# A streaming encoder layer: the sample's queries, keys and values of all head pairs multiplied ahead of attention

## The reference

```python
z = rms_norm(x, g) @ w_in          # q latent 256 | kv latent 128 | rotary key 32 | u 1024 | gate_a | gate_b
q = (rms_norm(c_q) @ w_q_b).reshape(b, t, 16, 96)            # 64 plain + 32 rotary per head
lat_all = concatenate([past_lat, rms_norm(c_kv)])
kv = (lat_all @ w_kv_b).reshape(b, n_k, 16, 128)             # 64 key + 64 value per head
k_nope, v = rms_norm(kv[..., :64]), kv[..., 64:]
attn = chunk_causal_mla(q_nope, q_rope, k_nope, kr_all, v)   # block-causal softmax attention
mixed = sigmoid(gate_a) * attn + sigmoid(gate_b) * rg_lru(conv(u))
x = x + mixed @ w_out
x = x + (silu(conv(gate)) * conv(val)) @ w_down              # gate, val = rms_norm(x) @ w_up
```

## Time and profile before

| | |
|---|---|
| median of 3 runs | 874.24 us (871.04 to 875.2) |
| profiled execution, span from first to last instruction | 872.8 us; the profile gives no other time of its own |
| busy: TensorE, VectorE, ScalarE, GpSimd | 852.5, 568.6, 365.7, 192.9 us |
| moved by DMA | 63.73 MB, 73 GB/s on average |

### The profile page before, as it was taken

One profiled execution on the slowest core, in us unless ns is written; L12 is line 12 of the kernel. 1 busy time (PEld: TensorE's weight loads), 2 busy tenths in 40 slices (PEclk: granted clock), 3 DMA queues, 4 the chain that ended last, 5 costly groups with the idle time before them and its releaser, 6 DMA issues.

```text
span 872.8 us, 16689 instructions
## 1 busy us (share of the span) xinstructions
PE 852.5 (98%) x6522; PEld 817.2 (94%) x6522; DVE 568.6 (65%) x998; ACT 365.7 (42%) x608; POOL 192.9 (22%) x206
## 2 busy tenths in 40 slices
PE   5999999899999999999999999999999999999998
PEld 5999898789999899877999999999999999999998
DVE  5586678867675676887656888778777876222121
ACT  5534959655655466556245221222212221122121
POOL 4021123202021121121140333323333234010000
PEclk8999999899999999999999999999999999999999
DMA  8433311131120101100223233232322323233321
GB/s 245 116 90 95 89 49 38 40 80 38 28 54 24 53 25 29 50 1 26 73 75 95 75 94 96 72 96 74 94 81 87 94 68 93 82 105 99 104 56 39
DMA packets 114466, 63.73 MB, mean 73 GB/s; under 512 B 7660, under 2 KB 112878, under 8 KB 114412
## 3 DMA queue, kind: packets, MB, share of 16 engines
q1 hardware_dynamic: 112428, 59.25, 24.0%
q0 software_dynamic: 1936, 3.70, 1.7%
q10 hardware_dynamic: 48, 0.02, 0.0%
HBM read 59.85 MB, written 2.70 MB: 72 GB/s over the span
## 4 chain that ended last, share of the span: by engine, by line
PE 88%; ACT 6%; DVE 3%; issue 2%; DMA 0%; POOL 0%; SPq 0%; ACTq 0%; DVEq 0%; POOLq 0%
PE PS L1612 49%; PE PS L1758 9%; PE PS L1841 6%; PE PS L1775 4%; PE PS L1813 4%; PE PS L1651 3%; PE PS L1717 2%; PE PS L1795 2%; PE PS L2045 2%; PE PS L1713 2%; PE PS L1749 2%; PE PS L1739 1%; PE PS L1680 1%; PE PS L1624 1%; PE PS L1820 1%
## 5 line engine op out<-in xcount | busy, mean ns | idle before, releaser
L668 ACT ACTIVATE w_hi<-w_raw 128x1024 fp32r<-128x1024 f32 (+2 forms) x102 | 105.5, 1035 | 316.5 <-PE PS L1612 301.4
L1101 DVE TENSOR_TENSOR w_lo<-w_raw,w_hi 128x1024 fp32r<-128x1024 f32 (+2 forms) x102 | 124.8, 1224 | 114.5 <-ACT w_hi L668 114.3
L1612 PE MATMUL PS<-x2h,w_hi 128*128 128x274 f32 x704 | 147.6, 291 | 0.0
L1612 PE MATMUL PS<-x2h,w_lo 128*128 128x274 f32 x704 | 147.0, 290 | 0.0
L1612 PE MATMUL PS<-x2l,w_hi 128*128 128x274 f32 x704 | 146.9, 290 | 0.0
L1612 PEld LDWEIGHTS PS<-x2l,w_hi 128*128 128x128 f32 x704 | 112.0, 189 | 0.0
L1612 PEld LDWEIGHTS PS<-x2h,w_hi 128*128 128x128 f32 x704 | 111.9, 189 | 0.1
L1612 PEld LDWEIGHTS PS<-x2h,w_lo 128*128 128x128 f32 x704 | 111.4, 189 | 0.0
L630 POOL TENSOR_TENSOR uct<-uct 128x548 f32<-128x548 f32 x22 | 30.2, 1373 | 176.4 <-DVE uct L1565 176.4
L1612 PE MATMUL PS<-hh,w_hi 128*128 128x274 f32 x308 | 64.7, 291 | 0.0
L1612 PE MATMUL PS<-hh,w_lo 128*128 128x274 f32 x308 | 64.6, 291 | 0.0
(11 more groups left out here) (291 smaller groups left out, 1851.2 us busy)
## 6 DMA issues: line engine op xcount, KB each, us to landing
w_raw<-in_w_up_dram SPq DMA_DIRECT2D x44, 512.0 KB, 3.9
w_raw<-in_w_in_dram SPq DMA_DIRECT2D x24, 512.0 KB, 3.9
w_raw<-in_w_down_dram SPq DMA_DIRECT2D x16, 512.0 KB, 4.3
w_raw<-in_w_out_dram SPq DMA_DIRECT2D x8, 512.0 KB, 4.3
w_raw<-in_w_down_dram SPq DMA_DIRECT2D x8, 384.0 KB, 4.0
xnat<-in_x_prompt_dram SPq DMA_DIRECT2D x4, 512.0 KB, 5.4
w_raw<-in_w_in_dram SPq DMA_DIRECT2D x4, 416.0 KB, 7.4
wq<-in_w_q_b_dram SPq DMA_DIRECT2D x8, 192.0 KB, 2.5
```

Source lines behind the costliest of these rows:

```text
L668: nc.scalar.activation(hi[:, slot % 2, 0:n], raw[:, slot % 4, 0:n], ACT.Copy).then_inc(s_hi, 1)
L1101: tt(lo[:, slot % 2, 0:n], raw[:, slot % 4, 0:n], hi[:, slot % 2, 0:n].bitcast(F32), ALU.subtract).then_inc(s_lo, 1)
L1612: last = mm(PS[:, 2 * rank + j, 0:HT], w[:, slot % 2, cols], x[:, k0 + k, j * HT:(j + 1) * HT], start=(k0 + k == 0 and first), stop=(k0 + ...
```

## The change

The sample's rows leave the tiles. TILES becomes (4, 4, 2, 2): two key units of four tiles, two query units of two, and two value units. In their place two calls of sample_qkv multiply the 32 sample rows by the weights of all pairs, the first call (r = 0) for pairs 0, 2, 4, 6, the second for the odd ones, four pairs at a time in column groups of 32. They stand in products g = 5 and g = 6; the keys and queries of pair 0 stay in g = 7 and 8. ScalarE evacuates each result and stores it to a new HBM tensor; before each pair it issues three DMAs that fetch the 32 rows into Kn, Qn and V. GpSimd clears the 96 other rows of the last tiles once.

```diff
-        TILES = (4, 4, 1, 2, 2, 1)
+        TILES = (4, 4, 2, 2)
+        NUNIT, NVU = 4, 2
 # SP
+            def sample_weights(r):
+                if r:
+                    sp.wait_ge(s_smul, r)
+                for k in range(NQ):
+                    sp.dma_start(swq[:, k, :, :], w_q_s[:, k, r]).then_inc(s_swin, 16)
+                sp.dma_start(swkv[:, :, :], w_kv_s[:, r]).then_inc(s_swin, 16)
             for t in range(I_IN, I_IN + 11):
                 w_in_item(t)
+                if t == I_IN + 5:
+                    sp.wait_ge(s_ss, NTT)
+                    sample_weights(0)
+            sample_weights(1)
 # GpSimd, after conv_tail(5)
+            pool.wait_ge(s_sst, 32)
+            for s in range(2):
+                nc.gpsimd.memset(Kn[s][0:LASTP, NKT - 1, :, :], 0.0)
+                nc.gpsimd.memset(Qn[s][0:LASTP, NT, :, :], 0.0).then_inc(s_sz, 1)
 # ScalarE
             def evacuate_kq(q, u, bank):
+                if u == 0:
+                    if q >= 2:
+                        act.wait_ge(s_tr, q * 5 - 5)
+                    else:
+                        act.wait_ge(s_sst, 32)
...
+                    act.dma_start(Kn[q % 2][LASTP:, NKT - 1, :, :], heads[:, 0]).then_inc(s_skq[q % 2], 16)
+                    act.dma_start(Qn[q % 2][LASTP:, NT, :, :].rearrange("p h n -> p (h n)"), rows_q[:, 0:2 * QK]).then_inc(s_skq[q % 2], 16)
+            def evacuate_sample(r):
+                act.wait_ge(s_smul, r + 1)
+                nc.scalar.activation(sqkv[:, r, 0:2 * QK], PS[:, 4, 0:2 * QK], ACT.Copy)
+                nc.scalar.activation(sqkv[:, r, 2 * QK:], PS[:, 5, 0:4 * NOPE], ACT.Copy).then_inc(s_sev, 1)
+                act.wait_ge(s_sev, r + 1)
+                act.dma_start(store[r], sqkv[:, r, :]).then_inc(s_sst, 16)
             def evacuate_v(q, u, bank):
+                if u == 0:
...
+                    act.dma_start(V[LASTP:, q % 2, NKT - 1, 0:3:2, :], heads[:, 1]).then_inc(s_svin[q % 2], 16)
 # ScalarE, squares_keys
+                act.wait_ge(s_skq[q % 2], 32 * (q // 2) + 32)
 # ScalarE, attend
-                    if kq and n < 3:
+                    if kq and n < 2:
                         evacuate_kq(p + 2, 2 * n, 0)
                         evacuate_kq(p + 2, 2 * n + 1, 1)
 # ScalarE, early stretch, after lru_exps (g == 5) and lru_mults (g == 6)
-                if 6 <= g < 9:
+                if 4 <= g < 6:
+                    evacuate_sample(g - 4)
+                if 6 <= g < 8:
                     for u in range(2):
                         evacuate_kq(0, 2 * (g - 6) + u, 4 + u)
...
-            for u in range(4, 6):
-                evacuate_kq(1, u, u - 4)
 # TensorE
+            def sample_qkv(r):
+                pe.wait_ge(s_swin, 48 * (r + 1))
+                for k in range(NQ):
+                    for g in range(4):
+                        mm(PS[g * DEC:(g + 1) * DEC, 4, 0:2 * QK], cqT[:, k, S0:S0 + DEC], swq[:, k, g, :],
+                           start=(k == 0), stop=(k == NQ - 1))
+                for g in range(4):
+                    last = mm(PS[g * DEC:(g + 1) * DEC, 5, 0:4 * NOPE], latT[:, SEQ + PAST:], swkv[:, g, :], start=True, stop=True)
+                last.then_inc(s_smul, 1)
 # TensorE, values
+                if n == 8:
+                    pe.wait_ge(s_svin[p % 2], 16 * (p // 2) + 16)
 # TensorE, attend
-                    if kq and n in (1, 2):
-                        for u in (2 * n, 2 * n + 1):
+                    if kq and n == 1:
+                        for u in (2, 3):
...
-                    for u in (1, 2):
...
-                        values_in(p + 1, u, (u + 1) % 2)
+                    values_in(p + 1, 1, 0)
 # TensorE, early stretch, before lru(g - 3)
+                if 5 <= g < 7:
+                    pe.wait_ge(s_sev, g - 4)
-                if 7 <= g < 10:
+                if 7 <= g < 9:
                     pe.wait_ge(s_kqf, 2 * (g - 6))
```

More of the change, by code:

```diff
@@ L172, in layer @@
         U = fixed("U", [P, KD, LEAD + T])
+        gates_at = place
         gates = fixed("gates", [P, 3, 2, T])
@@ L228, in layer @@
         lsq = at("lsq", [P, NTT, KVL + ROPE], zone + NTT * QL * 4)
+        NS = 2 * QK + 4 * NOPE
+        swq = at("swq", [P, NQ, 4, 2 * QK], kq_at[1])
+        swkv = at("swkv", [P, 4, 4 * NOPE], gates_at + 4 * T * 4)
+        sqkv = at("sqkv", [P, 2, NS], kq_at[0] + NKT * 2 * NOPE * 4)
+        assert kq_at[1] + NQ * 4 * 2 * QK * 4 <= wq_at and 4 * 4 * NOPE <= 2 * T and 2 * NS <= NTT * 2 * QK
+        assert kq_at[1] >= zone + NTT * (QL + KVL + ROPE) * 4
         mxh = at("mxh", [P, KD, T], xs, F32R)
@@ L331, in layer @@
         s_kq, s_kqf = sem("kq_product"), sem("kq_evacuated")
+        s_swin, s_smul, s_sev, s_sst = sem("sample_weights_in"), sem("sample_qkv_product"), sem("sample_qkv_evacuated"), sem("sample_qkv_stored")
+        s_sz = sem("sample_tiles_cleared")
+        s_skq = [sem(f"sample_kq{s}_in") for s in range(2)]
+        s_svin = [sem(f"sample_v{s}_in") for s in range(2)]
         s_v, s_vf = sem("v_product"), sem("v_evacuated")
@@ L345, in layer @@
         s_yt, s_yn, s_ysample = sem("y_transposed"), sem("y_natural"), sem("last_sample_natural")
+        store = nc.dram_tensor("sample_qkv_dram", (2, P, NS), F32, kind="Internal").ap()
         block = ctx.enter_context(nc.Block())
@@ L811, in evacuate_kq @@
             def evacuate_kq(q, u, bank):
-                act.wait_ge(s_kq, q * 6 + (u + 1))
-                if u == 0 and q >= 2:
-                    act.wait_ge(s_tr, q * 5 - 5)
+                if u == 0:
[3 more added lines that the diff above has]
+                        act.wait_ge(s_sst, 32)
+                    rows_q = store[q % 2, q // 2 * DEC:(q // 2 + 1) * DEC, :]
+                    heads = rows_q[:, 2 * QK:].rearrange("t (h c n) -> t c h n", h=2, c=2)
+                    act.dma_start(Kn[q % 2][LASTP:, NKT - 1, :, :], heads[:, 0]).then_inc(s_skq[q % 2], 16)
+                    act.dma_start(Qn[q % 2][LASTP:, NT, :, :].rearrange("p h n -> p (h n)"), rows_q[:, 0:2 * QK]).then_inc(s_skq[q % 2], 16)
+                act.wait_ge(s_kq, q * NUNIT + (u + 1))
                 tiles = TILES[u]
-                if u < 3:
+                if u < 2:
                     dst = Kn[q % 2][:, 4 * u:4 * u + tiles, :, :].rearrange("p t h n -> p (t h n)")
@@ L846, in evacuate_v @@
                     act.wait_ge(s_pv, q * 9 - 9)
[L847 to L850, removed]
+                if u == 0:
+                    heads = store[q % 2, q // 2 * DEC:(q // 2 + 1) * DEC, 2 * QK:].rearrange("t (h c n) -> t c h n", h=2, c=2)
+                    act.dma_start(V[LASTP:, q % 2, NKT - 1, 0:3:2, :], heads[:, 1]).then_inc(s_svin[q % 2], 16)
+                act.wait_ge(s_v, q * NVU + (u + 1))
+                dst = V[:, q % 2, 4 * u:4 * u + 4, 0:3:2, :]
+                nc.scalar.activation(dst, PS[:, bank, :].rearrange("p (t h n) -> p t h n", h=2, n=VD), ACT.Copy).then_inc(s_vf, 1)
             def value_ones(s):
@@ L1017, in _ @@
                 columns_left(0, v, 4 + v)
-            for u in range(3):
-                evacuate_v(0, u, (0, 1, 7)[u])
+            for u in range(NVU):
+                evacuate_v(0, u, u)
             exps(0, 0)
@@ L1745, in values_in @@
                     pe.wait_ge(s_wv[q % 2], 32 * (q // 2) + 32)
-                for a in range(TILES[u]):
-                    t = 4 * u + a
-                    k0 = t * P if t < NKT - 1 else NK - P
+                for a in range(4):
+                    k0 = (4 * u + a) * P
                     last = mm(PS[:, bank, a * P:(a + 1) * P], latT[:, k0:k0 + P], wkv[:, q % 2, 1, :], start=True, stop=True)
@@ L1909, in attend @@
                     if second and n == 8:
-                        pe.wait_ge(s_vf, 3 * (p + 1) + 1)
+                        pe.wait_ge(s_vf, NVU * (p + 1) + 1)
                         gate_half(second, 1)
                 if following:
-                    for u in (1, 2):
[L1914 to L1919, removed]
-                        values_in(p + 1, u, (u + 1) % 2)
+                    if second:
+                        pe.wait_ge(s_gf, 2 * (second - I_G) + 1)
+                    else:
+                        pe.wait_ge(s_trf, 4 * (p + 1) + 4)
+                    values_in(p + 1, 1, 0)
                 values(p, 8)
@@ L1927, in units @@
                     pe.wait_ge(s_lrui, min(g - 3, KD))
+                    if g < 7:
+                        sample_qkv(g - 5)
+                        return
                     for u in range(4) if g == NF - 1 else (2 * (g - 7), 2 * (g - 7) + 1):
                         keys_queries(int(g == NF - 1), u, 4 + u if g == NF - 1 else 4 + u % 2)
-                return units if 7 <= g < 10 or g == NF - 1 else None
+                return units if 5 <= g < 9 or g == NF - 1 else None
             pe.wait_ge(s_rs, 1)
@@ L1961, in _ @@
             pe.wait_ge(s_free, 11)
-            for u in (4, 5):
-                keys_queries(1, u, u - 4)
             for v in range(4):
```

(7 more changed lines are left out.)

37 lines of the change are left out of this document (19 added, 18 removed).

## The result

The changed kernel takes 880.88 us (median of 6 runs, 880.19 to 883.01), the kernel before beside it 874.12 (6 runs, 871.04 to 875.26): a ratio of 1.0089, 95% interval 1.0074 to 1.0105. It is slower by 6.8 us between the two medians; the interval of the ratio says 6.5 to 9.2 us. The profiled execution has a span of 878.4 us, 5.6 more than before.

What follows compares the result with a forecast made beforehand. TensorE, busy 852.5 of 872.8 us, seemed to bound the kernel, but ScalarE's work was expected to be waited for. Early stretch 5.4, pairs 1 to 5 3.5, other pairs -0.6: 8.3 us on 874.24 gives 882.5, range 871 to 888.

Steps and rivals of the forecast that it cites:

- early stretch: Everything up to attention's first exp: added products, evacuations and DMA issues cost 5.4 us, bounds 3.1 to 6.2.
- Pairs 1 to 5: Attention: TensorE stands still 1.8 us before the fifth score, awaiting ScalarE's chain; each pair 0.7 us longer, 3.5 in all.
- (1): Sixth product: the first sample_qkv call moves its end, the evacuation and ScalarE's next step by 1.1 us.
- (2): ScalarE behind lru_exps: the second sample evacuation and its DMA issue make lru(3) wait, 1.2 us in all.
- (3): evacuate_kq(0, 0) on ScalarE: two more DMA issues cost 0.9 us, making lru(4) 3.2 us late.
- (4): Ninth product: four query tiles instead of a key tile and two query tiles, 1.1 us more.
- (5): evacuate_kq(1, 0) before lru_mults: two DMA issues and four query tiles instead of two to evacuate, 0.9 + 0.2 us.
- the sign I had named: Start of attention: first exp near 160 us if the forecast holds, near 157 if it is wrong on the issues.
- TensorE's work decides: Rival, n = 1 to n = 3 of each pair: removed matmuls come through as time won, 867.6 us; chance 0.14.
- The clock: Rival: larger TensorE gaps, early and in five pairs, bring half speed; 12 us more, 894, or 885 to 888; chance 0.09.
- The groups run side by side: Denies the rival that sample_qkv's column groups run one after another, 6.6 us more in the early stretch, 889; chance 0.03.
- Half of each: Rival: early stretch at its lower bound, +3.1, pairs' gains and stalls in balance; 874.5 to 877 us, chance 0.16.

Runs made afterwards that it cites:

- e1: Changed kernel with tanh and split moved ahead of the evacuation of units 2 and 3 at n = 1, pairs 1 to 5: 872.82 us, ratio 0.9985.
- e2: Changed kernel with query unit 2 multiplied at n = 1 and unit 3 at n = 2, instead of both at n = 1: 873.7 us, ratio 1.0003.
- e3: Changed kernel without the 24 fetches of the sample's rows, which are set to zero: 881.29 us, ratio 1.0081.
- e6: Changed kernel with pair 0's units spread over three products and pair 1's unit 3 after the last product: 878.46 us, ratio 1.0045.
- e7: Changed kernel with the edits of e1, e2 and e6 together: 868.29 us, ratio 0.9936.
- e8: e7 with the first sample_qkv in the seventh product and the second in the tenth, its weights and store later: 867.51 us, ratio 0.9919.
- e5: Kernel before the change, with only tanh and split moved ahead of the evacuations at n = 1: 873.82 us, ratio 0.9996.

## Why the prediction was right

I gave 882.5 us, 871 to 888, and slower as the likeliest; it is 880.88. The kernel loses in the two places named. By places the loss is 6.6 us where I forecast 8.3, and some terms of the early stretch were priced too high. The runs as a whole (6.5 to 9.2 us) don't tell the two sums apart.

**Pairs 1 to 5: right, and shown.** Forecast: idle time of 1.8 us before the fifth score, +0.7 per pair, 3.5 in all. Found: 1.65 and 3.95 (0.74 in most pairs, 0.94 in the last). e1 and e2 show the mechanism from both sides. The margin of 0.19 us in the earlier trace rows said it: the removed work covered a chain. The fetches did fit into the gap of 0.94 us.

**Early stretch: 5.2 us forecast at the end of pair 0, 3.3 found.** (1) The first call: 1.1 forecast; from 82.56 to 83.84 it is 1.3, and lru(2) was 1.4 later. 24 instructions in 1.3 us show the column groups overlapping. On the changes of mode that the Trainium skill (TensorEngine Tiling (Array Packing), Key Properties) warns of, the trace has at most the 0.3 us by which that lies above my estimate; no run takes the changes of mode apart from the rest. (2) The second evacuation and its store behind the exps: 1.2 forecast, 1.0 found (first_tap is 2.4 us later, 95.49 against 96.92 plus the 0.98 of the starts, and the first call is 1.4 of that). lru(3) waits for the evacuation as forecast, but for 0.84 us where I had some 1.5. (3) **The step that failed**: "evacuate_kq(0, 0) issues two more, 0.9". They cost nothing (e3); lru(4) is 2.5 us late, not 3.2, and it is TensorE's own line, 3.9 late at lru(3), that sets it, not the wait for ScalarE that I had. (4) The two additional query tiles in the ninth product: 1.1 forecast, and lru(5) is another 1.1 later. e6 takes 1.3 back. (5) "0.9 + 0.2" at evacuate_kq(1, 0): the two issues at 144.49 and 144.84 lie under activations and hold ScalarE up by 0.13 us at most. In their place stood something I had not priced: ScalarE waited for pair 1's unit 3, with TensorE at its lower clock.

I had taken ScalarE's 0.46 us from the only row of that queue and let it decide five issues, 2.3 us in all. For the four of them that don't follow a wait on ScalarE's own last result the lower bound, nothing, was right or nearly so. Without those two terms of 0.9 the sum is 6.5 us, near the 6.6 found, but that agreement is luck: larger differences cancel. At the first exp 3.6 would be left and 4.35 were found, with 0.7 from the lower clock at 142 us. Pair 0 then gave 1.05 back where I had 0.2, since in the eight microseconds from the first exp on the clock stood at 0.64 and 0.94, and at 0.50 and 0.67 before. The pairs cost 0.45 more than forecast. By the sign I had named (first exp near 160, or near 157 if I am wrong on the issues) the result lies between: the first exp stands at 159.0 counted from the start before, 158.3 without the clock's 0.7.

The Trainium skill (DMA: Bandwidth & Descriptors, Issuing engines are not separate DMA queues) calls the sequencer's time for an issue usually small relative to the DMA. The trace agrees roughly: the fetches of Kn and Qn are issued in 0.31 to 0.44 us and land in 1.6 and 1.7. The size of an issue was not my mistake, then. The mistake was to add it to ScalarE's time, where it runs beside a table load or an activation.

**Rivals.** TensorE's work decides (867.6) is wrong for this kernel. Its mechanism holds in e7 and e8, where the chain is out of the way and the 1.1 us per pair come through; that their 868.29 and 867.51 lie so near its number is in part luck, since both also mend the early stretch. The clock: with idle times of 1.65 us in five pairs, the granted clock between 196 and 268 and between 300 and 336 us stays at 1.00, so that rival is refuted for pairs 1 to 5. The groups run side by side. Half of each would have needed the pairs to break even.

## What to carry to other kernels

Before taking work off a busy engine, find what that work covers: here 0.19 us of margin lay between a unit of matmuls and a chain of evacuation, tanh, split and exp on another engine, and removing 1.1 us of work cost 0.74 us per pair until the chain was reordered. A change that loses by a wait it uncovers may still beat the kernel it came from, once work that nobody waits for is moved out of the chain. Put DMA issues where an engine is still finishing earlier instructions, not behind a wait for its own last result. And compare single profiles place by place: two executions of the same work differed by 2.2 us in one stretch.

## What the hardware showed that I had not expected

**The cost of an issue depends on what stands ahead.** Under a table load or activations, two issues of 0.34 and 0.44 us cost ScalarE nothing (102.43 and 102.80; 0.13 us at most at 144.49 and 144.84). Behind a wait for the engine's own evacuation one leaves 0.40 us of idle time (at 96.92). The first is shown by e3; the second is read from the trace, and no run varied that wait alone.

**TensorE's clock differs between executions of nearly the same program.** In these windows the number after POOL's is the granted clock. From 142 to 144 us, first the changed kernel, then e3:

```profile
142.00:144.00 2.00, 2.00 (x12) 2.00 (x12) 2.00 (x4) 1.99 (x3) 1.40 (x2) 0.50 0.00 0
```

```profile
142.00:144.00 2.00, 1.90 (x17) 1.90 (x18) 2.00 (x5) 1.97 (x3) 0.45 (x1) 1.00 0.00 0
```

Both come out of the same idle time of 2.0 us ahead of L1762. In the changed kernel the clock then stands at 0.50 of full speed (the level of 1.2 GHz), and its 16 key instructions take 2.8 us where e3 needs 1.9, the 16 query instructions behind them 3.2 where e3 needs 2.5. ScalarE waits for the last of these (0.43 us at 147.50), and its lru_mults come 0.7 us later. At the start of attention, the kernel before and e5, whose work is the same up to there (the first exp stands 112.5 us behind the first product in both):

```profile
154.00:158.00 4.00, 3.19 (x10) 2.22 (x10) 3.84 (x6) 3.72 (x8) 0.00 (x0) 0.50 0.00 0
158.00:162.00 4.00, 4.00 (x21) 3.39 (x20) 1.17 (x3) 2.21 (x4) 0.00 (x0) 0.67 0.88 207
```

```profile
154.00:158.00 4.00, 4.00 (x29) 3.29 (x28) 3.43 (x4) 3.98 (x9) 0.00 (x0) 1.00 0.29 52
158.00:162.00 4.00, 3.96 (x27) 3.66 (x26) 3.37 (x14) 3.55 (x8) 0.00 (x0) 1.00 0.65 159
```

From first product to the end of pair 0, e5 takes 149.4 us and the kernel before 151.6. So 2.2 us of a span can come from one short stretch at the lower clock. The changed kernel, whose first exp comes at 158.02, lies between:

```profile
158.00:162.00 4.00, 3.56 (x15) 3.15 (x16) 4.00 (x5) 3.63 (x8) 0.00 (x0) 0.64 0.10 18
162.00:166.00 4.00, 4.00 (x25) 3.47 (x24) 1.94 (x6) 3.13 (x7) 0.00 (x0) 0.94 0.79 199
```

It happens behind the fifth score of pair 0 as well. After idle times of nearly 2 us there the clock stays at 1.00 in the changed kernel; in e3 it is 0.62 from 170 to 174 us, and the rest of pair 0 takes 27.6 us and not 26.3. So the early stretch's 3.3 us is a difference of two executions with different luck: counted from the first product, pair 0 ends at 154.9 us in the changed kernel and 156.3 in e3, at 151.6 in the kernel before and 149.4 in e5. The forecast's 5.2 us lies inside what these allow; only the places from the first product up to 141 us, where the clock is 1.00 in the changed kernel, the kernel before and e3, size single terms.

Why one execution is given the lower clock and another isn't stays open; no run varied the idle time ahead of it alone. With the first product's start (40.3 to 43.4 us in these profiles), this is why single profiles are compared place by place and the size of each gain is taken from the medians.
